# A decoder trunk's feed-forward blocks: the first chunk of three blocks computed with channels on partitions, and the other half of the bank for each pair's short matmul

## The reference

```python
D_MODEL, SEQ, D_FF = 1024, 256, 2816

def rms_norm(x, w):
    y = xf * lax.rsqrt(jnp.mean(xf * xf, axis=-1, keepdims=True) + NORM_EPS)
    return (y * w.astype(jnp.float32)).astype(x.dtype)

def swiglu_ffn(h, w_gate_up, w_down):
    gate, up = jnp.split(h @ w_gate_up, 2, axis=-1)
    return (jax.nn.silu(gate) * up) @ w_down
...
    for layer in range(DEPTH):
        h = h + 0.5 * swiglu_ffn(rms_norm(h, ffn1_norm[layer]), ffn1_w_gate_up[layer], ffn1_w_down[layer])
        hn = rms_norm(h, mix_norm[layer])
...
        h = h + 0.5 * swiglu_ffn(rms_norm(h, ffn2_norm[layer]), ffn2_w_gate_up[layer], ffn2_w_down[layer])
    return rms_norm(h, final_norm)
```

## Time and profile before

| | us |
|---|---|
| time, median of 3 runs | 1028.88 |
| lowest and highest | 1028.53, 1028.97 |
| the profiled execution | 1029.14 |
| its span, first to last instruction | 1027.4 |

### The profile page before, as it was taken

One profiled execution on the slowest core, in us unless ns is written; L12 is line 12 of the kernel. 1 busy time (PEld: TensorE's weight loads), 2 busy tenths in 40 slices (PEclk: granted clock), 3 DMA queues, 4 the chain that ended last, 5 costly groups with the idle time before them and its releaser, 6 DMA issues.

```text
span 1027.4 us, 15453 instructions
## 1 busy us (share of the span) xinstructions
PE 1016.9 (99%) x5790; PEld 881.5 (86%) x5790; DVE 675.4 (66%) x1005; ACT 569.1 (55%) x907; POOL 60.3 (6%) x120
## 2 busy tenths in 40 slices
PE   8999999999999999999999999999999999999997
PEld 7888888887888888888888888999999988888886
DVE  5766765576566776635766764688597666776733
ACT  7645543457565654536545543577567655554532
POOL 0000000110000000000000000404205100000000
PEclk9999999999999999999999999999999999999999
DMA  9666465343346555563665465343242347556521
GB/s 322 214 208 200 163 245 201 138 165 109 99 130 228 172 186 216 212 199 102 196 213 191 166 243 205 118 155 123 83 144 83 124 144 231 179 176 219 213 87 41
DMA packets 124308, 175.81 MB, mean 171 GB/s; under 512 B 7360, under 2 KB 97760, under 8 KB 124256
## 3 DMA queue, kind: packets, MB, share of 16 engines
q1 hardware_dynamic: 121552, 172.77, 49.5%
q10 hardware_dynamic: 2704, 2.33, 0.7%
HBM read 174.02 MB, written 1.06 MB: 170 GB/s over the span
## 4 chain that ended last, share of the span: by engine, by line
PE 97%; DVE 1%; ACT 1%; DMA 1%; issue 0%; SPq 0%; ACTq 0%; DVEq 0%
PE bank L1761 29%; PE bank L1691 15%; PE bank L1693 15%; PE bank L1692 14%; PE bank L1763 14%; PE bank L2085 2%; PE bank L2079 2%; PE bank L1988 1%; PE bank L1712 1%; PE bank L1923 1%; PE bank L1954 1%; PE bank L1853 1%; DMA w_raw<-in_ffn_w_gate_up 1%; DVE x_sb L1184 0%; PE bank L2182 0%
## 5 line engine op out<-in xcount | busy, mean ns | idle before, releaser
L1761 PE MATMUL bank<-xT,w_hi 128*128 128x512 f32 x1280 | 444.9, 394 | 0.0
L1147 DVE TENSOR_TENSOR w_lo<-w_raw,w_hi 128x2048 fp32r<-128x2048 f32 x152 | 347.4, 2290 | 105.7 <-ACT w_hi L727 105.0
L727 ACT ACTIVATE w_hi<-w_raw 128x2048 fp32r<-128x2048 f32 x153 | 294.0, 1930 | 118.0 <-PE bank L1693 118.0
L1763 PE MATMUL bank<-xT,w_lo 128*128 128x256 f32 x1280 | 354.8, 277 | 0.0
L1761 PEld LDWEIGHTS bank<-xT,w_hi 128*128 128x128 f32 x1280 | 240.0, 188 | 55.7
L1763 PEld LDWEIGHTS bank<-xT,w_lo 128*128 128x128 f32 x1280 | 240.4, 188 | 0.1
L1691 PE MATMUL bank<-w_hi,hT_hi 128*128 128x512 f32 x352 | 137.5, 391 | 0.0
L1693 PE MATMUL bank<-w_hi,hT_lo 128*128 128x512 f32 x352 | 137.0, 389 | 0.0
L1692 PE MATMUL bank<-w_lo,hT_hi 128*128 128x512 f32 x352 | 137.0, 389 | 0.0
L793 ACT ACTIVATE silu_g<-bank 128x256 f32<-128x256 f32 x80 | 26.4, 382 | 175.4 <-PE bank L1763 175.4
L1234 DVE TENSOR_TENSOR silu_g<-bank,silu_g 128x256 f32<-128x256 f32 x80 | 30.2, 419 | 119.5 <-ACT silu_g L793 119.5
(11 more groups left out here) (312 smaller groups left out, 1218.7 us busy)
## 6 DMA issues: line engine op xcount, KB each, us to landing
w_raw<-in_ffn_w_gate_up SPq DMA_DIRECT2D x170, 512.0 KB, 4.6
w_raw<-in_ffn_w_down SPq DMA_DIRECT2D x88, 512.0 KB, 4.0
w_raw<-in_gdn_w_in SPq DMA_DIRECT2D x32, 512.0 KB, 4.4
w_raw<-in_attn_w_in SPq DMA_DIRECT2D x12, 512.0 KB, 4.1
w_raw<-in_attn_w_out SPq DMA_DIRECT2D x8, 512.0 KB, 3.7
w_raw<-in_gdn_w_out SPq DMA_DIRECT2D x8, 512.0 KB, 3.6
w_raw<-in_ffn_w_gate_up SPq DMA_DIRECT2D x12, 256.0 KB, 6.1
x_sb<-in_x SPq DMA_DIRECT2D x4, 256.0 KB, 5.4
```

What stands on the lines that cost most here:

```text
L727: act.activation(w_hi[u0 % RING][:], w_raw[u0 % RING][:], ACT.Copy).then_inc(hi_ready, 1)
L1147: dve.tensor_tensor(w_lo[u0 % RING][:], w_raw[u0 % RING][:], w_hi[u0 % RING][:].bitcast(F32), ALU.subtract).then_inc(split_ready, 1)
L1761: pe.matmul(banks[m][:], w[0], xT[:, kt, :, :].rearrange("p s n -> p (s n)"), start=(kt == 0), stop=False, skip_group_check=True)
L1763: z = pe.matmul(banks[m][:, SEQ:2 * SEQ], w[1], xT_hi[:, kt, :], start=False, stop=(kt == KT - 1), skip_group_check=True)
```

## The change

Three things are changed.

1. In blocks 1, 2 and 3, chunk 0 is computed with channels on partitions too (`entered_chunk`): 96 matmuls of 256 columns into banks 2 and 3 in place of 48 of 512, in the order of the GDN's first units, with `early_hi` and `early_lo` at these entries as well. `rstd` is transposed (`transposed_rstd`, into bank 1) before the last quarter of the chunk's second unit, and the four transposes of the result in chunk 1 go away. VectorE multiplies by `rstd_rows`, ScalarE applies silu, VectorE multiplies by the up half. Chunks 1 and 2 of these blocks join the loop, which has five rounds there. The banks are laid out anew: `CHUNKS`, `acc_of` and `enter_bank`.
2. In every pair of `gate_chunk` the short matmul adds to columns 0 to 255 of the bank, no longer to 256 to 511 (`channel_step`). What ScalarE copies and VectorE adds is the same two halves as before.
3. The GDN uses `transposed_rstd` as well, so two transposes stand where two float32 matmuls stood.

```diff
+BY_HALVES = {2: 0, 3: 1, 4: 2, 5: 3}
...
-        ENTER_BANKS = {0: (4, 6), 1: (4, 2), 2: (4, 2), 3: (4, 6), 5: (4, 2)}
-        FIRST_CHUNK = [(2, 3), (6, 7), (2, 3), (6, 7)]
-        CHUNKS = [[(6, 7, 0, 1), (2, 3, 4, 5)], [(0, 1, 2, 3), (4, 5, 6, 7)],
-                  [(6, 7, 0, 1), (2, 3, 4, 5)], [(0, 1, 2, 3), (4, 5, 6, 7)]]
+        ENTER_BANKS = {0: (4, 6), 1: (4, 2)}
+        FIRST_CHUNK = (2, 3)
+        CHUNKS = [(2, 3, 4, 5), (6, 7, 0, 1)]
         ACC = [(6, 7), (0, 1)]
         ATT_ACC = [(6, 0), (7, 1)]
-        FFN_ACC = [(2, 0), (3, 1)]
-        ACC_OF = [None, ACC, ATT_ACC, FFN_ACC, ACC, ACC, FFN_ACC]
+        ROWS_BANK = 1
+
+
+        def acc_of(e):
+            return ATT_ACC if e == E_FFN[1] else ACC
...
+            if e in E_FFN[1:]:
+                return bank[((4, 5), (acc_of(e)[0][0], acc_of(e)[1][0]), (4, 4), (5, 5))[n][j // 2]][:, j * P:(j + 1) * P]
             return bank[ENTER_BANKS[e][t] + half][:, j * P:(j + 1) * P]
 
-        def chunk_banks(f, j):
-            return [bank[b] for b in CHUNKS[f][0 if j % 2 else 1]]
+        def chunk_banks(j):
+            return [bank[b] for b in CHUNKS[j % 2]]
...
-        def rounds(eng, body):
-
-            body(0)
-            with eng.Fori(1, (NCH - 1) // 2) as i:
+        def rounds(eng, f, body):
+
+            if f == 0:
+                body(0)
+            with eng.Fori(1 if f == 0 else 0, (NCH - 1) // 2) as i:
...
+            def copy_rows(n, b):
+
+                act.wait_ge(rows_psum, n)
+                act.activation(rstd_rows[:], bank[b][:, 0:TT * P].rearrange("p (t n) -> p t n", t=TT),
                                ACT.Copy).then_inc(rows_ready, 1)
...
-                act.wait_ge(rstd_ready, RSTD_FFN[f])
-                first_chunk(f)
-                if f == 0:
+                if f:
+                    copy_rows(ROWS_FFN[f], ROWS_BANK)
+                    act.wait_ge(g_scaled, NCH * f)
+                    act.activation(silu_g[0][:], silu_g[0][:], ACT.Silu).then_inc(g_silu, 1)
+                    split_hi(u + 4)
+                    act.wait_ge(h_cols, NCH * f)
+                    act.activation(hT_hi[:, 0:BANK], h_row[0][:].rearrange("p m n -> p (m n)"),
+                                   ACT.Copy).then_inc(hT_hi_ready, 1)
+                    split_hi(u + 5)
+                else:
+                    act.wait_ge(rstd_ready, RSTD_FFN[0])
+                    first_chunk()
...
-                if e == E_GDN and js[-1] < 2:
-                    dve.wait_ge(early_hi, n + 1)
+                if e in BY_HALVES and js[-1] < 2:
+                    dve.wait_ge(early_hi, 2 * BY_HALVES[e] + n + 1)
...
-                if e == E_GDN:
+                if e in BY_HALVES:
...
-                first_chunk(f)
+                if f:
+                    dve.wait_ge(rows_ready, ROWS_FFN[f])
+                    dve.wait_ge(unit_done, u + 2)
+                    dve.tensor_tensor(silu_g[0][:], bank[FIRST_CHUNK[0]][:].rearrange("p (m n) -> p m n", m=2),
+                                      rstd_rows[:].rearrange("p t n -> p (t n)").unsqueeze(1).broadcast_to([P, 2, SEQ]),
+                                      ALU.mult).then_inc(g_scaled, 1)
+                    dve.wait_ge(g_silu, NCH * f)
+                    dve.scalar_tensor_tensor(h_row[0][:], bank[FIRST_CHUNK[1]][:].rearrange("p (m n) -> p m n", m=2), 0.5,
+                                             silu_g[0][:], ALU.mult, ALU.mult).then_inc(h_cols, 1)
+                    split_lo(u + 4)
+                    dve.wait_ge(hT_hi_ready, NCH * f + 1)
+                    dve.tensor_tensor(hT_lo[:, 0:BANK], h_row[0][:].rearrange("p m n -> p (m n)"),
+                                      hT_hi[:, 0:BANK].bitcast(F32), ALU.subtract).then_inc(hT_lo_ready, 1)
+                    split_lo(u + 5)
+                else:
+                    first_chunk()
...
+            def channel_step(u0, kt, banks):
+
+                for m in range(4):
+                    w = ring(u0, slice(kt % 4 * BANK + m * P, kt % 4 * BANK + (m + 1) * P))
+                    pe.matmul(banks[m][:], w[0], xT[:, kt, :, :].rearrange("p s n -> p (s n)"),
+                              start=(kt == 0), stop=False, skip_group_check=True)
+                    z = pe.matmul(banks[m][:, 0:SEQ], w[1], xT_hi[:, kt, :], start=False,
+                                  stop=(kt == KT - 1), skip_group_check=True)
+                return z
...
+            def transposed_rstd(n, b):
+
+                pe.wait_ge(rstd_ready, n)
+                for t in range(TT):
+                    z = pe.transpose(bank[b][:, t * P:(t + 1) * P], rstd[:, t:t + 1].broadcast_to([P, P]), ident[:])
+                z.then_inc(rows_psum, 1)
+
+            def entered_chunk(f):
+
+                e, u = E_FFN[f], U_FFN[f]
+                for kh in range(2):
+                    wait_split(pe, u + kh)
+                    for q in range(4):
+                        if kh and q == 3:
+                            transposed_rstd(RSTD_FFN[f], ROWS_BANK)
+                        if q < 3:
+                            pe.wait_ge(early_lo, 6 * BY_HALVES[e] + 3 * kh + q + 1)
+                        else:
+                            pe.wait_ge(xT_lo_ready, 4 * e + 2 * kh + 2)
                         kt = 4 * kh + q
                         for m in range(4):
-                            w = ring(u0, slice(q * BANK + m * P, q * BANK + (m + 1) * P))
-                            pe.matmul(banks[m][:], w[0], xT[:, kt, :, :].rearrange("p s n -> p (s n)"),
-                                      start=(kt == 0), stop=False, skip_group_check=True)
-                            z = pe.matmul(banks[m][:, SEQ:2 * SEQ], w[1], xT_hi[:, kt, :], start=False,
-                                          stop=(kt == KT - 1), skip_group_check=True)
-                    z.then_inc(unit_done, 1)
-                    if j == 1 and kh == 0 and not looped(i):
-                        first_transposes(f)
-
-            def first_transposes(f):
-
-
-                pe.wait_ge(rstd_ready, RSTD_FFN[f])
-                pe.wait_ge(h_ready, TT * (f + 1))
-                for t in range(TT):
-                    z = pe.transpose(bank[FIRST_CHUNK[f][0]][:, t * P:(t + 1) * P], rstd[:, t:t + 1].broadcast_to([P, P]),
-                                     ident[:])
-                z.then_inc(rows_psum, 1)
+                            z = products(bank[FIRST_CHUNK[m // 2]][:, m % 2 * SEQ:(m % 2 + 1) * SEQ],
+                                         ring(u + kh, slice(q * BANK + m * P, q * BANK + (m + 1) * P)),
+                                         (xT_hi[:, kt, :], xT_lo[:, kt, :]),
+                                         start=(kt == 0 and m % 2 == 0), stop=(kt == KT - 1), skip_group_check=True)
+                        if q == 3:
+                            z.then_inc(unit_done, 1)
+                        elif kh == 0 and q < 2:
+                            enter(e, 2 + q)
+                pe.wait_ge(rows_ready, ROWS_FFN[f])
...
+            def first_transposes():
+
+
+                pe.wait_ge(h_ready, TT)
+                transposed_rstd(RSTD_FFN[0], FIRST_CHUNK[0])
...
-                for kh in range(2):
-                    in_unit(U_FFN[f] + kh, 0, kh, FIRST_CHUNK[f], E_FFN[f])
-                if f == 0:
+                if f:
+                    entered_chunk(f)
+                else:
+                    for kh in range(2):
+                        in_unit(kh, 0, kh, FIRST_CHUNK, E_FFN[0])
...
-            def rstd_in_rows():
-
-                pe.wait_ge(rstd_ready, RSTD_GDN)
-                for t in range(TT):
-                    z = pe.matmul(bank[7][:, t * P:(t + 1) * P], rstd[:, t:t + 1].broadcast_to([P, P]), ident[:],
-                                  start=True, stop=True)
-                z.then_inc(rows_psum, 1)
-
             def entered_channel_unit(u0, kh, banks):
 
                 wait_split(pe, u0)
                 for j in range(4):
                     kt = 4 * kh + j
                     if kh and j == 3:
-                        rstd_in_rows()
+                        transposed_rstd(RSTD_GDN, 7)
```

More of the change, by code:

```diff
@@ L763, in enter_hi, with first_chunk, first_hT_hi @@
                             z.then_inc(xT_hi_ready, 1)
-                        elif e == E_GDN and n < 2 and j == 1:
+                        elif e in BY_HALVES and n < 2 and j == 1:
                             z.then_inc(early_hi, 1)
-            def first_chunk(f):
-                u = U_FFN[f]
-                act.wait_ge(unit_done, u + 2)
+            def first_chunk():
+                act.wait_ge(unit_done, 2)
                 for t in range(TT):
-                    act.activation(silu_g[0][:, t, :], bank[FIRST_CHUNK[f][t]][:, 0:FC], ACT.Silu,
+                    act.activation(silu_g[0][:, t, :], bank[FIRST_CHUNK[t]][:, 0:FC], ACT.Silu,
                                    scale=rstd[:, t:t + 1]).then_inc(silu_ready, 1)
-                split_hi(u + 4)
-                split_hi(u + 5)
```

(34 more changed lines are left out.)

43 lines of the change are left out of this document (22 added, 21 removed).

## The result

| | us |
|---|---|
| before, median of 5 runs | 1028.59 (1028.48 to 1028.97) |
| after, median of 5 runs | 1033.83 (1033.18 to 1035.56) |
| ratio | 1.005, 95% interval 1.0038 to 1.0061 |
| the profiled execution after, and its span | 1033.40, 1031.7 |

A forecast was written before the change was run, and what follows sets the result against it. TensorE's matmul list, busy 1016.9 of 1027.4 us, was taken as the bound. Chunk 0 stages (-0.77) and GDN (-0.22) sum to -0.99 us, the rest zero: 1027.9 us, range 1027.0 to 1029.3.

The forecast's parts named there:

- The entries and the stage: Chunk 0 of blocks 1 to 3: no entry wait, stage 12.86 us as at the GDN; 0.77 us gained in all.
- What is newly waited for: TensorE's stops in chunk 0 for `rstd` and ScalarE's row copy: covered by 0.46 and 0.86 us, cost nothing.
- The loop: Entry now before chunk 1 in blocks 1 to 3: under 0.6 us, hidden by 0.86 us of cover, cost nothing.
- The other half of the bank: New address for the short matmul in 1280 pairs: zero, bounds 6.4 us either way at 5 ns per pair.
- The GDN: Two transposes for `rstd` in place of four instructions there: 0.22 us less.
- the price of a pair: Gate chunks: a 512-column and a 256-column matmul together take 0.35 us, 0.23 + 0.12, unchanged by the edit.
- The sign that I had named: Chunks of 32 pairs: the forecast is wrong if one differs from 11.1 us.
- The rival of a slower pair: All 1280 pairs: the bank half matters and each loses 5 ns, giving 1034.3 us; chance 0.03.

The follow-up runs named there:

- e3: The changed kernel with chunks 1 and 2 of blocks 1 to 3 written out ahead of the loop, still without transposes in chunk 1: 1033.61 us, ratio 1.005.
- e1: The kernel before with only the short matmul of all 1280 pairs moved to columns 0 to 255: 1028.52 us, ratio 0.9999.
- e2: The changed kernel with the short matmul put back to columns 256 to 511, the rest kept: 1033.51 us, ratio 1.0048.
- e9: The changed kernel with one idle transpose between chunk 0 and chunk 1 of blocks 1 to 3: 1027.70 us, ratio 0.9992.
- e15: The changed kernel with one idle 256-column matmul between chunk 0 and chunk 1 of blocks 1 to 3: 1034.31 us, single execution.
- e14: The kernel before with two idle transposes added to the six inside chunk 1 of all four blocks: 1031.42 us, single execution.
- e16: The changed kernel with ScalarE's copy of the rows held until chunk 0 is complete, so TensorE stands still ahead of chunk 1: 1036.56 us, single execution.

## Why the prediction was wrong

**The entries and the stage: right.** Forecast 0.23 to 0.25 us from the last matmul to the first and 12.8 to 12.9 us for the stage; measured 0.24 and 12.85 in all three blocks. Taking the GDN's stage as the model, less two transposes, was exact.

**What is newly waited for: right.** The root ended at 295.94, 0.46 us before the transposes at 296.40, and the copied rows at 297.21, 0.84 before the first pair. TensorE stood nowhere in chunk 0.

**The loop: right.** Its first pair follows at 0.12 us, and e3 shows the same time without it.

**The other half of the bank: right, and measured** (e1, e2). A pair did become slower, by 6.7 ns where I had 5 as the bound, but not from this cause.

**The GDN: right**, 0.24 us against 0.22.

**The step that failed** is the price of a pair, 0.35 us from the earlier trace rows, carried from chunks behind the transposes to chunks without them. It stood in the sum as a constant, "the lengths add up exactly", and so into the step that took the removal of four transposes from chunk 1 for 0.44 us of work and nothing else. 960 pairs hung on it: 6.7 ns for 912 of them are 6.1 us, six times the gain. The trace of before had the counterexample right behind the stage that I replaced whole: the 16 pairs from 298.43 to the transposes at 304.07 take 5.64 us, 352.5 ns for a pair. I read that stretch only by its ends and its transposes, and the steady chunks at two pairs with a last digit of 10 ns, where 347 and 353 both print as 0.35. The sign that I had named, a chunk of 32 pairs other than 11.1 us, is what came: an eighth of 90.46 is 11.3. The rival of a slower pair gave the right size (1034.3) with a cause that isn't there, at a chance of 0.03, and was left out of the range; that its number came so near is luck. The runs put in place of the constant two rates, 346.7 and 353.4 ns, chosen by what TensorE does just ahead of the stream. Why a given break leads to the one or the other stays open.

## What to carry to other kernels

Here a dense stream of matmuls had more than one steady rate with the same instructions and the same operands. Before a stream is taken as a constant, measure its rate over a hundred or more repeats, and do so in each place where something else stands before it. When an edit removes or adds small matmuls next to a long regular stream, compare the stream's rate first, and try an edit with one idle small matmul before it is given up: here that turned a loss of 5.2 us into a gain of 1. A difference in a run with many repeats is worth looking at down to the nanosecond: 6.7 ns for a pair were the whole result. And an idle instruction that sets the rate is fragile: one and three ahead of the stream, and one and two inside it, gave different answers, so the rate has to be measured again after each edit near it.

## What the runs showed of the hardware

- A pair of a 512-column and a 256-column matmul on new weights each took 346.7 ns or 353.4 ns at the full granted clock, steady over at least 256 pairs and over the loop's jumps. The slow one repeats after three pairs (0.35, 0.35 and 0.36 us, 1.06 in all); three fast ones take 1.04.
- Which one comes is decided at the start of the stream. It is not the half of the bank (e1, e2), not the loop (e3), not the number of instructions alone (e9 against e15, block 0 against block 1 in e14), and a standstill of 1.04 us did not bring the fast one (e16). In every run blocks 1 to 3, which have the same work just ahead of their pairs, had the same rate. What in TensorE keeps the phase stays open; no run here looked inside it.
- One idle transpose takes 0.03 us itself (298.00 to 298.03 in e9), and the pair behind it takes 0.43 us (298.03 to 298.46) where 0.35 is usual, so it costs 0.11 in all.
